# The second expert stage in halves of 1408 columns, down one half behind

## The reference, cut to what matters

```
logits = xt @ router_w
top_logits, top_idx = lax.top_k(logits, TOP_K)          # TOP_K = 2
top_w = jax.nn.softmax(top_logits, axis=-1)
xs = xt[tok]                                            # tokens sorted by expert
h  = jax.nn.silu(ragged_dot(xs, w_gate, sizes)) * ragged_dot(xs, w_up, sizes)
ys = ragged_dot(h, w_down, sizes) * top_w[...]
out = segment_sum(ys, tok, num_segments=n_tok)
x = layernorm(ALPHA * x + (1 + g2) * out)
```

## Time and profile before

| | |
|---|---|
| median of 3 runs | 2105.48 us |
| profiled execution | 2103.75 us |
| its span | 2101.8 us |
| second expert stage, first to last weight product | 1353.43 to 2078.81 us |
| one expert (1441.48 to 1983.50 us holds six) | 90.3 us |
| granted PE clock, mean over the span | 0.975 |

### The profile page before, as it was taken

How to read it: one execution, slowest core, us unless ns; L and a number is a source line. 1 busy time by engine, 2 the same in 40 slices (tenths; PEclk the granted TensorE clock), 3 DMA queues, 4 the chain that set the end, 5 groups by cost and what they waited for, 6 DMA issues and landing times.

```text
span 2101.8 us, 67959 instructions
## 1 busy us (share of the span) xinstructions
PE 1978.3 (94%) x31065; PEld 1600.3 (76%) x31065; DVE 637.4 (30%) x1407; ACT 194.8 (9%) x320; POOL 18.9 (1%) x69
## 2 busy tenths in 40 slices
PE   6999999999999989999999999889899998999996
PEld 4787577877777757758676675689898998989895
DVE  4686332322322232354224424501011010101104
ACT  2002110000000011000000110201010101010100
POOL 1000000000000000000000000000000000000000
PEclk9999999999999999999999999899999999999998
DMA  9998659999999993346667433299999999999992
GB/s 352 312 390 312 236 203 420 420 421 421 425 422 421 420 360 137 114 168 256 246 235 259 144 117 119 84 394 360 394 382 384 379 380 396 368 395 381 378 387 92
DMA packets 245811, 655.77 MB, mean 312 GB/s; under 512 B 17364, under 2 KB 38260, under 8 KB 237556
## 3 DMA queue, kind: packets, MB, share of 16 engines
q1 hardware_dynamic: 237216, 647.41, 81.1%
q0 software_dynamic: 1456, 5.24, 0.7%
q10 hardware_dynamic: 7076, 2.20, 0.5%
HBM read 653.76 MB, written 1.05 MB: 312 GB/s over the span
## 4 chain that ended last, share of the span: by engine, by line
PE 81%; DMA 11%; DVE 4%; SPq 2%; issue 1%; DVEq 0%; ACT 0%
PE ps L1672 80%; DMA ring<-in_moe_w_up_dram 10%; PE ps L1680 2%; SPq L446 1%; DMA ring<-in_w_ada_dram 1%; DVE stat L1043 0%; DVE arena L1245 0%; DVE hT L931 0%; DVE x L1152 0%; DVE tok L918 0%; DVE tok L1151 0%; DVE newton L911 0%; DVE hT L1026 0%; DVE x L1037 0%; DVE arena L1117 0%
## 5 line engine op out<-in xcount | busy, mean ns | idle before, releaser
L1672 PE MATMUL ps<-arena,ring 128*64 128x80 f32 (+2 forms) x25216 | 883.7, 232 | 51.5 <-DMA ring<-in_moe_w_up_dram 46.0
L1672 PEld LDWEIGHTS ps<-arena,ring 128*64 128x64 f32 (+1 forms) x25216 | 869.8, 139 | 73.8 <-DMA ring<-in_moe_w_up_dram 49.9
L1672 PE MATMUL ps<-hT,ring 128*128 128x256 f32 (+1 forms) x1680 | 359.4, 384 | 4.1 <-DVE stat L935 2.2
L1672 PEld LDWEIGHTS ps<-hT,ring 128*128 128x128 f32 (+1 forms) x1680 | 308.4, 188 | 50.9 <-issue 4.8
L1672 PE MATMUL ps<-ring,arena 128*64 128x512 f32 (+1 forms) x880 | 273.8, 595 | 1.5 <-DVE stat L1580 1.1
L1672 PE MATMUL ps<-arena 128*128 128x128 f32 (+7 forms) x1296 | 227.5, 342 | 12.1 <-DVE arena L1517 5.6
L1672 PEld LDWEIGHTS ps<-ring,arena 128*64 128x64 f32 (+1 forms) x880 | 104.5, 159 | 150.8 <-issue 147.2
L1672 PEld LDWEIGHTS ps<-arena 128*128 128x128 f32 (+4 forms) x1296 | 156.0, 189 | 63.8 <-issue 43.7
L1402 DVE TENSOR_TENSOR arena<-arena,ps 128x160 f32<-128x160 f32 x88 | 28.3, 321 | 534.6 <-PE ps L1672 534.6
L1672 PE MATMUL ps<-ring,hT 128*128 128x512 f32 (+2 forms) x256 | 87.6, 500 | 0.0
L1304 DVE TENSOR_TENSOR x<-x,ps 128x512 f32<-128x512 f32 x104 | 71.6, 688 | 31.1 <-PE ps L1672 31.1
(11 more groups left out here) (323 smaller groups left out, 741.7 us busy)
## 6 DMA issues: line engine op xcount, KB each, us to landing
ring<-in_moe_w_gate_dram SPq DMA_DIRECT2D x160, 512.0 KB, 10.0
ring<-in_moe_w_up_dram SPq DMA_DIRECT2D x160, 512.0 KB, 7.1
ring<-in_moe_w_down_dram SPq DMA_DIRECT2D x160, 512.0 KB, 10.2
ring<-in_w_gate_dram SPq DMA_DIRECT2D x32, 2048.0 KB, 14.2
ring<-in_w_up_dram SPq DMA_DIRECT2D x32, 2048.0 KB, 13.6
ring<-in_w_down_dram SPq DMA_DIRECT2D x32, 2048.0 KB, 12.3
ring<-in_w_in_dram SPq DMA_DIRECT2D x19, 2048.0 KB, 14.1
ring<-in_w_ada_dram SPq DMA_DIRECT2D x12, 2048.0 KB, 15.4
```

The costliest lines, as they stand in the source:

```text
L1672: ins = pe.matmul(*args, **kw)
```

## The change

- The hidden width is cut into two halves of 1408 columns (`FH`, 11 tiles `TH`). The ring's room is laid out as 4 rows of 1408 columns for gate (`held_gate`), 4 for up (`held_up`) and 11 rows of 1024 columns for down (`held_down`).
- Gate and up of a half are made in two quarters of 4 row tiles (`KQ`): gate quarter, up quarter, gate quarter, up quarter, as one loop body run twice (`half_in`). They add into PSUM banks that DVE has cleared.
- Down of a half (`half_down`) comes after gate and up of the next half. It no longer waits for silu and product of what PE has just made.
- SP issues each row tile by itself, 8 transfers of 704 KB for each quarter pair and 11 of 512 KB for a half's down: 54 for an expert, in place of 63. Gate and up now have 5632 bytes to a row. The down rows are issued between the two quarter pairs. PE frees each row tile by itself (`piece_used`).
- The moving rows of a quarter are copied by ACT to `x_rows`, one row tile behind the other.
- The side work stands together at the end of an expert's two halves, on banks 6 and 7.
- `half_in(0)`, `half_in(1)` and `half_down(1)` stand written out ahead of the loop over experts, and `half_down(16)` behind it.
- The path for experts with over 80 tokens (`second_all`) is rewritten likewise; it is not taken.

The diff, cut to its core; lines that stay are shown where they are needed:

```diff
-UNITS = F2 // CH
-TAIL = F2 - UNITS * CH
-PIECES = 4
-FREES = 2 * PIECES + 1
+FH = F2 // 2
+TH = FH // P
+KQ = KD // 2
+QUARTER = KQ * FH
+BANK_TILES = 6
+PER_HALF = 4 * KQ + TH
+def used_by(n, k):
+    first = isinstance(n, int) and n == 0
+    return n * PER_HALF + (k + 1 - (0 if first else TH))
...
-SIDE2 = (0, 1, 2, 3, 0, 1, 2, 3, 0)
-UP_BANKS = (7, 3)
+SIDE2 = (6, 7, 6, 7, 6, 7, 6, 7, 6)
+GATE_BANK, UP_BANK, Y_BANK = 0, 2, 4
...
+        gated2 = view(0, TH * CAP2)
+        hid2 = view(1024, TH * CAP2)
+        x_rows = view(2048, KQ, CAP2)
...
+        flat = ring[:, :, :].rearrange("p s n -> p (s n)")
+        GATE_AT, UP_AT, DOWN_AT = 0, QUARTER, 2 * QUARTER
+        held_gate = flat[:, GATE_AT:UP_AT].rearrange("p (k n) -> p k n", k=KQ)
+        held_up = flat[:, UP_AT:DOWN_AT].rearrange("p (k n) -> p k n", k=KQ)
+        held_down = flat[:, DOWN_AT:DOWN_AT + TH * D].rearrange("p (f n) -> p f n", f=TH)
...
+            def load_quarter(w, e, v, q, at, place, full, n):
+                for j in range(KQ):
+                    if n is None:
+                        left_by_ring(at + (j + 1) * FH)
+                    else:
+                        use = j + (at // QUARTER) * KQ
+                        sp.wait_ge(piece_used, used_by(n, use) if q else used_by(n - 1, 2 * KQ + use))
+                    sp.dma_start(place[:, j, :], expert_cols(w, e, v * FH, FH)[:, q * KQ + j, :]).then_inc(full[j], 16)
+            def load_quarters(e, v, q, n):
+                load_quarter(wg, e, v, q, GATE_AT, held_gate, gate_row, n)
+                load_quarter(wu, e, v, q, UP_AT, held_up, up_row, n)
...
+            def load_downs(e, v, n):
+                for f in range(TH):
+                    if n is None:
+                        left_by_ring(DOWN_AT + (f + 1) * D)
+                    else:
+                        sp.wait_ge(piece_used, used_by(n - 1, 4 * KQ + f))
+                    sp.dma_start(held_down[:, f, :], expert_rows(wd, e, v * FH, FH)[:, f, :]).then_inc(down_row[f], 16)
...
+            load_quarters(0, 0, 0, None)
+            load_downs(0, 0, None)
+            for place, full, w, first in ((held_gate, gate_row, wg, 0), (held_up, up_row, wu, KQ)):
+                for j in range(KQ):
+                    sp.wait_ge(piece_used, first + j + 1)
+                    sp.dma_start(place[:, j, :], expert_cols(w, 0, 0, FH)[:, KQ + j, :]).then_inc(full[j], 16)
+            for q in range(2):
+                load_quarters(0, 1, q, 1)
             with sp.Fori(1, NE2) as e:
+                load_quarters(e, 0, 0, e * 2)
+                load_downs(e - 1, 1, e * 2)
+                load_quarters(e, 0, 1, e * 2)
+                load_quarters(e, 1, 0, e * 2 + 1)
+                load_downs(e, 0, e * 2 + 1)
+                load_quarters(e, 1, 1, e * 2 + 1)
+            load_downs(NE2 - 1, 1, 2 * NE2)
...
+                    def silu(used):
+                        act.wait_ge(piece_used, used)
+                        for b, (at, n) in enumerate(bank_spans(CAP2)):
+                            ins = act.activation(gated2[:, at:at + n], ps[:, GATE_BANK + b, 0:n], ACT.Silu)
+                        ins.then_inc(q["silu_done"], 1)
+                    def next_rows(c, up_used):
+                        for k in range(KQ):
+                            act.wait_ge(piece_used, up_used + k)
+                            act.activation(x_rows[:, k, :], xT[:, c * KQ + k, 0:CAP2], ACT.Copy).then_inc(rows_ready, 1)
+                    def new_rows(i):
+                        act.wait_ge(q["side_free"], side_op(i, 2) + 1)
+                        act.activation(x_rows, xT[:, 0:KQ, 0:CAP2], ACT.Copy).then_inc(rows_ready, KQ)
+                        act.wait_ge(q["side_free"], side_op(i, 3) + 1)
+                    new_rows(START)
+                    next_rows(1, KQ + 1)
+                    silu(3 * KQ)
+                    next_rows(0, 3 * KQ + 1)
+                    next_rows(1, used_by(1, KQ))
+                    silu(used_by(1, 3 * KQ - 1))
+                    new_rows(0)
+                    with act.Fori(1, NE2) as i:
+                        next_rows(1, used_by(i * 2, KQ))
+                        silu(used_by(i * 2, 3 * KQ - 1))
+                        next_rows(0, used_by(i * 2, 3 * KQ))
+                        next_rows(1, used_by(i * 2 + 1, KQ))
+                        silu(used_by(i * 2 + 1, 3 * KQ - 1))
+                        new_rows(i)
...
+                def clear(bank, done):
+                    for b, (_, n) in enumerate(bank_spans(cap)):
+                        ins = dve.memset(ps[:, bank + b, 0:n], 0.0)
+                    ins.then_inc(done, 1)
+                def gates_taken(n):
+                    dve.wait_ge(q["silu_done"], n + 1)
+                    clear(GATE_BANK, gate_clear)
+                def product(used):
+                    dve.wait_ge(piece_used, used)
+                    for b, (at, n) in enumerate(bank_spans(cap)):
+                        dve.tensor_tensor(hid2[:, at:at + n], gated2[:, at:at + n], ps[:, UP_BANK + b, 0:n], ALU.mult)\
+                           .then_inc(q["hid_ready"], 1)
+                def up_taken(n):
+                    dve.wait_ge(q["hid_ready"], n * 2 + 2)
+                    clear(UP_BANK, q["up_full"])
+                def y_taken(i):
+                    for half in range(2):
+                        ks = slice(4 * half, 4 * half + 4)
+                        ins = dve.tensor_tensor(yT[:, ks, :], ps[:, Y_BANK + half, 0:4 * cap]
+                                                .rearrange("p (a b) -> p a b", a=4),
+                                                gate_col[:, ks].unsqueeze(2).to_broadcast([P, 4, cap]), ALU.mult)
+                    ins.then_inc(q["y_free"], 1)
+                    dve.wait_ge(q["y_free"], i + 1)
+                def clear_y():
+                    dve.memset(ps[:, Y_BANK:Y_BANK + 2, 0:4 * cap], 0.0).then_inc(y_clear, 1)
...
+                build_pick(1)
+                gates_taken(0)
+                product(4 * KQ)
+                up_taken(0)
+                gates_taken(1)
+                moved(0)
+                product(used_by(1, PER_HALF - 1))
+                up_taken(1)
+                weighted(0)
+                build_pickw(1)
+                with dve.Fori(1, NE2) as i:
                     build_pick(i + 1)
+                    gates_taken(i * 2)
+                    product(used_by(i * 2, PER_HALF - 1))
+                    up_taken(i * 2)
+                    y_taken(i - 1)
+                    clear_y()
+                    gates_taken(i * 2 + 1)
                     slotted(i)
+                    moved(i)
+                    product(used_by(i * 2 + 1, PER_HALF - 1))
+                    up_taken(i * 2 + 1)
+                    for c in range(4):
+                        added(i, c, 4)
+                    weighted(i)
                     build_pickw(i + 1)
+                dve.wait_ge(piece_used, used_by(2 * NE2, PER_HALF - 1 - 4 * KQ))
+                y_taken(NE2 - 1)
...
+                def quarter(w, full, n, kk, bank):
+                    for k in range(KQ):
+                        pe.wait_ge(rows_ready, n * (2 * KQ) + (kk * KQ + (k + 1)))
+                        pe.wait_ge(full[k], n * 32 + (kk * 16 + 16))
+                        for f in range(TH):
+                            at = f % BANK_TILES * cap
+                            for c in range(2):
+                                last = mm(ps[c * HALF:(c + 1) * HALF, bank + f // BANK_TILES, at:at + cap],
+                                          w[:, k, f * P + c * HALF:f * P + (c + 1) * HALF], x_rows[:, k, :],
+                                          start=False, stop=(k == KQ - 1), skip_group_check=True)
+                        last.then_inc(piece_used, 1)
                     return last
+                def half_in(n):
+                    with pe.Fori(0, 2) as kk:
+                        pe.wait_ge(gate_clear, n + 1)
+                        quarter(held_gate, gate_row, n, kk, GATE_BANK)
+                        pe.wait_ge(q["up_full"], n + 1)
+                        quarter(held_up, up_row, n, kk, UP_BANK)
+                def half_down(n, y_cleared):
+                    pe.wait_ge(y_clear, y_cleared)
+                    for f in range(TH):
+                        pe.wait_ge(down_row[f], n * 16)
+                        if f % BANK_TILES == 0:
+                            pe.wait_ge(q["hid_ready"], n * 2 + (f // BANK_TILES - 1))
+                        for dt in range(KD):
                             for c in range(2):
+                                last = mm(ps[c * HALF:(c + 1) * HALF, Y_BANK + dt // 4, (dt % 4) * cap:(dt % 4 + 1) * cap],
+                                          held_down[:, f, dt * P + c * HALF:dt * P + (c + 1) * HALF],
+                                          hid2[:, f * cap:(f + 1) * cap], start=False, stop=(f == TH - 1),
+                                          skip_group_check=True)
```

(71 more changed lines are left out.)

291 lines of the change are left out of this document (111 added, 180 removed).

## The result

| | before | after |
|---|---|---|
| median | 2105.42 us (2102.23 to 2106.89, 4 runs) | 2091.88 us (2091.04 to 2094.6, 4 runs) |
| profiled execution, its span | 2103.75, 2101.8 us | 2094.6, 2092.9 us |
| second expert stage | 725.4 us | 716.7 us (1351.0 to 2067.7) |
| granted PE clock, mean over the span | 0.975 | 0.974 |

The account below looks back on a forecast made before the run. The weight stream was the bound, PE close under it; after the change PE, by little. 591.4 + 5.1 + 80.5 + 4.2 + 23 us gave a 704.2 us stage, 21.2 us gained, so 2083 us; 8 in 10 for 2054 to 2118 us.

Parts of the forecast that it names:

- The price of long rows: Weight transfers: a row of 5632 B takes 221 ns; an expert's stream takes 84 us (412 GB/s).
- The rival that it stays at 393 GB/s: Weight stream: long rows bring nothing, the stage takes 719 us and the kernel 2099 us; chance 0.10.
- the packet's fixed part: DMA packets: each costs a fixed 13.9 ns plus 36.7 ns per 1000 B.
- The loop's code is held: Expert loop: PE keeps its 1508 matrix instructions without fetching each pass; the rival, code not held, had chance 0.16.
- The two new side waits: Side work: PE waits 0.4 us for dispatch's first bank and some 2 us for the third combine product.
- 8448 products: Second expert stage: 16 halves x 528 weight products at 70 ns on PE, 591.4 us.
- side work, seven passes at full clock: Expert loop: side work on PE of 11.5 us in each of seven passes, 80.5 us.
- boundaries and quarters paced by the stream: Expert loop: leftover waits between PE and stream of 0.6 us in each of seven passes, 4.2 us.
- Part 2: Waits for up: buffers keep PE and stream going, neither waits long for the other; 0.6 us an expert left.
- the slow clock (1.6 us): PE in each expert: 1.6 us lost to the slow clock, claimed to go with the long waits.
- the stand of 6 us: After the side work: the stream waits about 6 us for PE's first freed row, then catches up.
- the code stalls: PE's code that runs once, before the loop: 10 stalls of 2.3 us, 23 us; no-stall rival chance 0.17.

Follow-up runs that it names:

- experiment 3: The changed kernel with each gate and up row tile loaded as two transfers, rows of 2816 bytes in place of 5632: 2113.14 us, ratio 1.0054.
- experiment 5: The changed kernel with nine small needless products on PE ahead of the third combine product, where it waited: 2079.57 us, ratio 0.9889.
- Experiment 2: The changed kernel with DVE's four additions and the weights' copy ahead of the product with up and the clears: 2070.38 us; again, 2072.66 us.
- Experiment 1: The changed kernel without the four combine products and their additions in the expert loop's seven passes (work left out): 2053.85 us, ratio 0.9753.
- experiment 6: The changed kernel with transposes, combine and weights behind the even half's down, dispatch behind the odd half's, additions early on DVE: 2086.4 us, ratio 0.9912.
- Experiment 7: On top of Experiment 2, transposes and dispatch moved ahead of the odd half's down, combine and weights left behind it: 2075.06 us, ratio 0.9871.
- experiment 4: The changed kernel with the first two halves of gate and up as one loop of two passes: 2096.14 us, ratio 0.9976.
- its twin: On top of Experiment 2, the first two halves of gate and up as one loop of two passes: 2074.43 us, ratio 0.9856.

## Why the prediction was right and wrong

**Right.** The direction and the mechanism of the gain: the long waits for up are gone, and PE sets the pace in five of the six parts of a pass. The price of long rows: in the window at 1569.50 us the engines were busy for 13.70 x 16 x 1.019 us; over the 1014 packets that are not small that is 220 ns each, and the forecast had 221. The stream alone needs 83.6 us a pass, the forecast 84 us. The rival that it stays at 393 GB/s falls by this, and experiment 3 shows that the packet's fixed part is real. The loop's code is held: its 1508 matrix instructions ran for 580 us with one packet. The Trainium skill's "Runtime: NRT & Kernel Launch", section Instruction fetch mechanics, gives PE room for 2048 instructions, and the trace agrees. Its two pages of 16 KiB, with a stall at a taken branch out of them, do not fit this trace, and the measurement decides. The two new side waits are where they were put, 0.34 and 1.78 us.

**Wrong: a gain of 12.5 us less in the stage.** By the terms of the sum:

| term | forecast | measured | |
|---|---|---|---|
| 8448 products | 591.4 us | 585.6 | -5.8 |
| side work, seven passes at full clock | 80.5 | 83.8 | +3.3 |
| slow clock behind it | 0 | 12.5 | +12.5 |
| boundaries and quarters paced by the stream | 4.2 | 15.7 | +11.5 |
| stalls of new code, and the clock behind them | 23 | 15.3 | -7.7 |
| side work of expert 0 | 5.1 | 4.1 | -1.0 |

(The prediction's 2082 us and 1.7 us are 2083.7, which it rounds to 2083.) The measured column is worked out from the segments of the trace: a quarter pair or a down at full pace takes 12.2 us (69.2 ns a product), and side work at full clock is that of experiment 5, 12.1 us six times and 11.2. The rows add up to 717.0 us, 0.3 more than the stage, by rounding.

*The first step that failed* is in Part 2: "the slow clock (1.6 us) goes with the long waits". The prediction itself put a wait of 2 us into each pass's side work, and rows 7 had shown what follows a wait of that size. Carried through, its own 1.6 us a pass would have been 11.2 us. Experiment 5 shows it alone: same wait, filled, and 12 us fewer; the six passes give 9.1 us of it and the last down 3.1. Experiment 2 takes the wait away and gets both, 3.3 us a pass.

*The second* is in Part 2 as well: "each waits for a place freed 10 us or more before ... So neither side waits long for the other". The places are not free for 10 us: SP issues each row within 0.3 us of PE's freeing its place. For each 12.2 us of PE's work the stream needs 13.9 (34.6 MB in six such parts, 83.6 / 6), so it falls 1.7 us behind in each. In the pass from 1773 to 1861 us the time from issue to landing grows from 3.9 us, for the first row behind the side work, to 12.5 us, for the last row of the odd half's second quarter pair; at full pace PE wants a place back after 10.9. So the odd second quarter pair takes 14 us. Then the side work frees no place for 12 us and more, the stream works off what is late and stands (0.16 of a share), and begins anew. The prediction saw the stand of 6 us but took the stream's catching up to be free. Experiment 1 gives the floor (side work shorter, that pair 16.5 us), experiment 6 breaks the six parts in two threes and the pair drops to 12.4 us: its rows land 3 us or more ahead of PE. Experiment 7 puts its two parts on either side of one down, and the pair stays at 14. The lateness is read from the landings. That what counts is the number of parts in a row is argued from these three, not shown by one run that changes it alone.

*Mis-sized the other way:* the code stalls. The count was right, 9 for 10, but one is 0.35 to 2.28 us, 1.3 on average, not 2.3. Against the 23 us stand 11.5 us in stalls; of the other 3.8 us of the 15.3 a slow clock behind the 2.28 us (0.90 on average from 1376.4 to 1393.4 us) is 1.5: in the run of experiment 5 that quarter pair has stalls as long and a clock of 1.00, and takes 15.6 us in place of 17.1. The rest stays open. What removing one is worth stays open too: in experiment 4 and its twin, stalls were saved and the stage was no shorter by over 0.2 us. Side work at full clock was 12.1 us for 11.5, or 3.3 us in seven: a gap of 0.87 us with no releaser, behind the weight transposes, was not in the sum. What it waits for is not shown. It's not the step back to the loop's start by itself: in experiment 6 there is no such gap where dispatch stands last ahead of that step.

## What to carry to other kernels

When a change takes one wait away and makes a smaller one, price the smaller one with everything that the old one drew behind it, the clock included; and on an engine that serves in order, put what the bottleneck waits for first: moving four additions and a copy ahead of a product and two clears was worth some 20 us here, more than the change itself. When a stream of transfers and the engine that uses it take nearly the same time, don't compare only their totals. The engine's pauses stop the stream too, as no buffer comes free. So add up how late the stream gets between two pauses, and set it against the time by which the buffers let it run ahead.

## What was unexpected of the hardware

PE's clock fell to 1.2 GHz behind a wait of 1.78 us in some passes and not in others of the same program, with nothing different in the rows of the timeline ahead. 2 us of needless products in that wait kept it at 2.4 GHz in all of them. A packet's time went with its length by a fixed part and a slope: a fit from mean lengths of 2393 and 7482 bytes gave the 117 ns of 2816 bytes and, within 1 ns, the 220 ns of 5632. Stalls of new code come about 127 matmuls (254 matrix instructions) apart where they follow each other closely, and their length varies from 0.35 to 2.28 us while the DMA engines are about equally full (shares of 1.02, 1.02, 0.99 and 1.02 over the four segments with the longest).
